# The MLP's input forms and low parts on VectorE, its quarters loaded at other times

## What is computed

```python
xn = rmsnorm(x, norm_mix_g)
z = xn @ w_in                                  # q | k | v | u | gate
attn_out = sink_attend(q, k, v, ...)           # windows of 128, chunks of 64
lru_out = gelu(gate) * rglru(u, ...)           # causal conv, then a scan
h = x + concat(attn_out, lru_out) @ w_out
hn = rmsnorm(h, norm_ffn_g)
y = h + square(relu(hn @ w_up)) @ w_down
y_out = rmsnorm(y, final_norm_g)
```

## Time and profile before

| | |
|---|---|
| median of three runs | 2179.25 us (2178.5 to 2181.05) |
| profiled execution | 2178.8 us |
| its span | 2177.0 us |
| PE busy | 1991.7 us, 91% |
| PEld busy | 1887.9 us, 87% |
| DVE busy | 1535.1 us, 71% |
| ACT busy | 1012.1 us, 46% |
| POOL busy | 498.3 us, 23% |
| chain that ended last | PE 63%, DVE 11%, issue 9%, POOL 7%, DMA 5%, ACT 3% |
| DRAM traffic over the span | 375.36 MB read, 123.68 MB written, 229 GB/s |

### The profile page before, as it was taken

How to read it: one execution, slowest core, us unless ns; L and a number is a source line. 1 busy time by engine, 2 the same in 40 slices (tenths; PEclk the granted TensorE clock), 3 DMA queues, 4 the chain that set the end, 5 groups by cost and what they waited for, 6 DMA issues and landing times.

```text
span 2177.0 us, 34222 instructions
## 1 busy us (share of the span) xinstructions
PE 1991.7 (91%) x11669; PEld 1887.9 (87%) x11669; DVE 1535.1 (71%) x2167; ACT 1012.1 (46%) x1967; POOL 498.3 (23%) x411
## 2 busy tenths in 40 slices
PE   6789889988898689999999889999999899999994
PEld 6778678777786489999999889999999799999994
DVE  7767777677679678878887866666666756666663
ACT  5555544644644355555555444433335433343431
POOL 3536565555666310100000401000002100000000
PEclk9889999999998799999999999999999899999997
DMA  6767677666755289988999887768878667777771
GB/s 176 222 175 230 179 220 227 199 218 186 239 176 172 77 305 308 320 289 289 344 324 293 267 279 245 231 204 264 270 222 270 225 197 218 216 216 216 219 213 63
DMA packets 396538, 500.91 MB, mean 230 GB/s; under 512 B 27498, under 2 KB 301450, under 8 KB 396394
## 3 DMA queue, kind: packets, MB, share of 16 engines
q1 hardware_dynamic: 394698, 493.38, 72.7%
q0 software_dynamic: 1696, 5.67, 0.8%
HBM read 375.36 MB, written 123.68 MB: 229 GB/s over the span
## 4 chain that ended last, share of the span: by engine, by line
PE 63%; DVE 11%; issue 9%; POOL 7%; DMA 5%; ACT 3%; SPq 1%; POOLq 0%; DVEq 0%; ACTq 0%
PE results L2065 19%; PE scores_a L2065 13%; PE tail L2065 13%; PE results L1849 9%; PE aux L2065 7%; DVE w_lo L1399 2%; PE aux L1969 1%; DMA s_scratch<-w_hi 1%; POOL xrow L930 1%; POOL prob L961 1%; DVE w_lo L1524 1%; POOL xrow L932 1%; POOL xrow L934 1%; DMA out<-hid_y 1%; POOL third L932 1%
## 5 line engine op out<-in xcount | busy, mean ns | idle before, releaser
L1081 ACT ACTIVATE w_hi<-w_raw 128x512 fp32r<-128x512 f32 (+1 forms) x360 | 241.0, 691 | 395.0 <-PE results L2065 174.8
L1524 DVE TENSOR_TENSOR w_lo<-w_raw,w_hi 128x512 fp32r<-128x512 f32 (+1 forms) x360 | 293.6, 829 | 49.9 <-ACT w_hi L1081 49.4
L1849 PE MATMUL results<-xg_hi,w_hi 128*128 128x448 f32 (+1 forms) x560 | 215.0, 384 | 27.4 <-DVE w_lo L1399 21.4
L1849 PE MATMUL results<-xg_lo,w_hi 128*128 128x448 f32 (+1 forms) x560 | 202.6, 362 | 0.0
L1849 PE MATMUL results<-xg_hi,w_lo 128*128 128x448 f32 (+1 forms) x560 | 202.4, 361 | 0.0
L2065 PE MATMUL results<-hn_hi,w_hi 128*128 128x348 f32 x576 | 189.4, 329 | 13.3 <-DVE hcur L1734 8.0
L1017 ACT ACTIVATE w_hi<-raw 128x1024 fp32r<-128x1024 f32 x110 | 116.3, 1058 | 167.3 <-PE results L1849 162.8
L1399 DVE TENSOR_TENSOR w_lo<-raw,w_hi 128x1024 fp32r<-128x1024 f32 x110 | 158.1, 1437 | 48.2 <-ACT w_hi L1017 48.0
L2065 PE MATMUL results<-hn_hi,w_lo 128*128 128x348 f32 x576 | 187.6, 326 | 0.0
L2065 PE MATMUL results<-hn_lo,w_hi 128*128 128x348 f32 x576 | 187.5, 326 | 0.0
L2065 PE MATMUL scores_a<-hn_hi,w_hi 128*128 128x348 f32 x480 | 156.3, 326 | 4.6 <-DVE hn_lo L1514 2.8
(11 more groups left out here) (275 smaller groups left out, 5726.1 us busy)
## 6 DMA issues: line engine op xcount, KB each, us to landing
w_lo<-s_scratch SPq DMA_DIRECT2D x128, 512.0 KB, 4.4
w_hi<-s_scratch SPq DMA_DIRECT2D x256, 256.0 KB, 3.6
w_raw<-in_w_up SPq DMA_DIRECT2D x144, 256.0 KB, 4.6
w_raw<-in_w_down SPq DMA_DIRECT2D x144, 256.0 KB, 4.3
raw<-in_w_in SPq DMA_DIRECT2D x70, 512.0 KB, 5.0
w_raw<-s_raw SPq DMA_DIRECT2D x64, 512.0 KB, 5.6
s_scratch<-w_lo SPq DMA_DIRECT2D x64, 512.0 KB, 5.8
s_scratch<-w_hi SPq DMA_DIRECT2D x128, 256.0 KB, 6.0
```

What stands on the lines that cost most here:

```text
L1081: nc.scalar.activation(ring(w2_hi, u, ks[0], len(ks)), raw_slots(u, ks[0], len(ks)), ACT.Copy)\
L1524: nc.vector.tensor_tensor(w2_lo[u.s][:, PHYS[ks[0]]:PHYS[ks[0]] + len(ks), :], raw_slots(u, ks[0], len(ks)), ring(w2_hi.bitcast(F32), u, k ...
L1849: last = nc.tensor.matmul(out, wt, x(kx), start=(start and i == 0 and part == 0), stop=(stop and i == len(ks) - 1 and part == 2))
```

## The change

- **Engine.** `input_form` goes from POOL to DVE for all three blocks, and so do low parts 6 and 4. POOL keeps nothing of `hn`. The semaphore `hn_lo_p` goes; `hn_lo_v` counts seven low parts, in the order 0 to 6.
- **Last mixing block, SP and POOL.** Quarters 0, 3 and 1 are loaded at q = 7, after that unit's sums have been moved, and quarter 2 at q = 8 as before. A unit's sums are now moved ahead of its quarter loads. Sum store 5 is issued at n = 18 instead of 17; sums step 5 is made after round 2's scaling instead of round 1's.
- **Last mixing block, DVE.** The two halo copies are left out there. In the four pairs of output halves stand form c (pair c), low part c - 1 (from pair 1 on), and weight low parts of unit 0 in pairs 2 and 3. Low parts 3 to 6 follow in unit 0.
- **Blocks 0 and 1, SP.** Quarters 0, 1 and 2 are loaded after products 0, 3 and 5 of unit 29, each one alone; quarter 3 (in `held`) at product 0 of unit 30, with the waits for unit 29's hidden parts.
- **Blocks 0 and 1, DVE.** Form 0 stands in unit 30, forms 1 to 3 and low parts 0 and 1 in unit 31, low parts 2 to 6 in unit 0 of the next block.
- **ACT.** High parts in the order 0, 5, 3, 1, 2, 6, 4; 0, 5 and 3 in unit 30, the others in unit 31.

```diff
-IORD = (0, 1, 2, 3, 6, 4, 5)
+IORD = (0, 5, 3, 1, 2, 6, 4)
...
-              "last": {9: 0, 11: 1, 12: 2, 15: 3, 16: 4, 17: 5}}
+              "last": {9: 0, 11: 1, 12: 2, 15: 3, 16: 4, 18: 5}}
...
-            "last": {"ix0": (0,), "ix1": (1, 2), "scan": (3, 4), 1: (5,)}}
+            "last": {"ix0": (0,), "ix1": (1, 2), "scan": (3, 4), 2: (5,)}}
...
-                    if blk.last and q == 6:
+                    move_sums(blk, n)
+                    if blk.last and q == 7:
                         sp.wait_ge(freed, 2 + uses + Z1)
                         sp.wait_ge(lru_lo, blk.before(2) + 2)
-                        for k in (0, 1, 3):
+                        for k in (0, 3, 1):
                             sp.dma_start(hn_slot(k), h_quarter(h_dram, 0, k)).then_inc(hn_in[k], 16)
                     if blk.last and q == 8:
                         sums_stored(blk)
                         sp.dma_start(hn_slot(2), h_quarter(h_dram, 0, 2)).then_inc(hn_in[2], 16)
-                    move_sums(blk, n)
...
-                if i == 30 and k == 0:
-                    last_up = Unit(UN * (b - 1) + 29)
-                    sp.wait_ge(prod_done, last_up.product(6))
-                    sp.wait_ge(hid_lo_done, hid_split(last_up.n, 5))
-                    sp.wait_ge(t_done, 3 * last_up.n + 2)
+                if i == 29 and k in (0, 3, 5):
+                    q = {0: 0, 3: 1, 5: 2}[k]
                     for h in range(2):
                         sp.wait_ge(ht_out[h], 16 * KT * b)
-                    for q in (0, 3, 2, 1):
-                        sp.dma_start(hn_slot(q), h_quarter(hn_dram[b - 1], 0, q)).then_inc(hn_in[q], 16)
+                    sp.dma_start(hn_slot(q), h_quarter(hn_dram[b - 1], 0, q)).then_inc(hn_in[q], 16)
+                if i == 30 and k == 0:
+                    n = Unit(UN * (b - 1) + 29).n
+                    sp.wait_ge(hid_lo_done, hid_split(n, 5))
+                    sp.wait_ge(t_done, 3 * n + 2)
+                    sp.dma_start(hn_slot(3), h_quarter(hn_dram[b - 1], 0, 3)).then_inc(hn_in[3], 16)
...
-                if u.i == 0:
-                    for k in hn_low_pool(u.b):
-                        input_low(u.b, k)
...
-                link(nc.vector.tensor_copy(kT[:, 0:CHUNK], kT[:, end:end + CHUNK]))
-                nc.vector.tensor_copy(vT[:, 0:CHUNK], vT[:, end:end + CHUNK]).then_inc(halo_done, 1)
+                if not blk.last:
+                    link(nc.vector.tensor_copy(kT[:, 0:CHUNK], kT[:, end:end + CHUNK]))
+                    nc.vector.tensor_copy(vT[:, 0:CHUNK], vT[:, end:end + CHUNK]).then_inc(halo_done, 1)
...
-                    if blk.last and couple == 2:
-                        weights_low(0, 0)
-                    if blk.last and couple < 3:
-                        input_low(0, IORD[couple])
+                    if blk.last:
+                        if couple >= 2:
+                            weights_low(0, couple - 2)
+                        input_form(0, couple)
+                        if couple >= 1:
+                            input_low(0, couple - 1)
...
                 if u.i == 0:
-                    input_low(u.b, 3)
-                    input_low(u.b, 5)
+                    for k in range(2 if u.b else 3, 7):
+                        input_low(u.b, k)
```

99 lines of the change are left out of this document (45 added, 54 removed).

## The result

The changed kernel takes 2145.55 us, median of three runs (2143.62 to 2146.69), against 2179.25: a ratio of 0.9843, interval 0.982 to 0.9865, or 33.7 us less. The forecast was 2141, its range 2133 to 2153. The profiled execution is the slowest of the three, 2146.7 us with a span of 2144.9.

A forecast was written before the change was run, and what follows sets the result against it. PE, the busiest engine, was taken to lose time only at three places where the MLP gets its input. Gains 19 + 12 + 9 = 40, less 1.5, gave 38.5 off 2179.25: 2141 us, range 2133 to 2153.

The forecast's parts named there:

- A1: Last mixing block: reordered sums and quarter loads remove PE's wait for POOL's scaling and the slow clock; gain 9.6 us.
- no wait for POOL's scaling above 2 us: Sign at the last mixing block: PE never waits more than 2 us for POOL's scaling of the probabilities.
- A2: Last mixing block: forms off POOL and no halo copy cut PE's 9.06 us wait to about 1; gain 8.
- A form on DVE: Length of an input form on DVE: bounds 1.60 and 3.40 us, 1.60 taken; at 3.40 the pairs lose 5 us.
- A3: Last mixing block's output halves, with moved DVE work: 21.0 us instead of 22.6, gain 1.5; 0 if the clock falls.
- Unit 0: After the last sum: doesn't move; a start of product 6 other than 21 us behind it would show the prediction wrong.
- B: End of block 0, units 30 to 32: 14.9 us lost, 2.5 to 3 of them stay; gain 12.
- the landing of the store of high parts: End of block 0: taken 2 us over the 6.0 median, so that ACT no longer makes DVE late.
- rival 1: New waits on quarter or store loads, unit 29 on or last mixing block, 0 to 4 us each: 2149; chance 0.17.
- The laying-out of forms and low parts in DVE's order: End of block 0: delays of 0.4 us before product 6, and 1 each at products 0 and 1 of unit 32.
- three signs: End of block 0: ACT's store wait below 2 us, PE's waits 3 us in sum, clock at its upper level.
- C: End of block 1: of 11.7 us lost, 0.65 + 1.0 + 1.1 stay; gain 9.

The follow-up runs named there:

- e4: The kernel before with only the changed order of sums, stores and quarter loads in the last mixing block; 2169.2 us.
- e5: The changed kernel with sum step 5 made behind round 1's scaling again instead of round 2's; 2149.1 us.
- e3: The changed kernel with the four input forms back on GpSimd in the last mixing block alone; 2155.1 us.
- e2: The changed kernel with the two halo copies of the last mixing block back; 2143.5 us.
- e0: The changed kernel run again without any edit, on the same chip as e12; 2147.5 us.
- e9: The changed kernel with the residual's loads moved from the start of unit 0 to behind its product 4; 2144.4 us.
- e12: As e7, with three weight loads of unit 32 behind unit 31's stores (block 0), residual's loads behind unit 0's first store; 2141.9 us.
- e7: As e1, with form 0 also moved on DVE from unit 30 to behind unit 31's first two additions; 2147.0 us.
- e1: The changed kernel with ACT's input high parts 5 and 3 behind all weight high parts in unit 30; 2150.0 us.
- e6: As e1, with all four quarters loaded at product 0 of unit 30 and high part 0 behind the weight high parts; 2152.1 us.

## Why the prediction was right, and where its sizes were off

**What bounds, and A1.** Right in place and size: 9.6 us forecast, 9.6 in the profile, 9.5 in e4 alone. Its sign, no wait for POOL's scaling above 2 us, was wrong all the same: the 2.30 us of the last round stood there before too. One bound was too tight: the landing of the step's data took 7.2 us as the upper end, and e5 measured 9.0. That did no harm, since the loads went out at 701.37 and POOL found the data there at 709.96, "by 711" as the sum has it.

**A2.** Right: 8 forecast, 8.2 measured. It is POOL's doing: e3 brings back 5.1 of it, and the copy beside a form, which e3 doesn't have, made up the 3.1 left. The prediction booked these 3.1 us to leaving the copies out; by e2 that gives nothing once the forms are away.

**A form on DVE** takes 1.60 us, the value taken; the other end of 3.40 was needed nowhere.

**A3.** The failed step is the clock: the sum took the output halves at the upper level, since only 1 us of wait was left in front; for a fall of the clock it had put the gain at 0. Busy time and clock of the stretch (length, busy us of PE, PEld, DVE, ACT, POOL, granted clock, DMA share, GB/s):

```profile
724.00:732.00 8.00, 4.70 (x27) 3.05 (x25) 7.59 (x20) 2.75 (x13) 1.73 (x2) 1.00 0.23 79
732.00:736.00 4.00, 2.09 (x11) 1.27 (x12) 2.82 (x7) 2.15 (x5) 0.35 (x1) 0.84 0.00 2
736.00:740.00 4.00, 4.00 (x12) 3.56 (x11) 1.03 (x1) 1.18 (x1) 0.00 (x0) 0.50 0.36 86
740.00:744.00 4.00, 4.00 (x18) 3.63 (x18) 1.25 (x2) 0.63 (x1) 0.00 (x0) 0.80 1.05 277
```

After the last rounds, in which PE is busy for about half of the time, the first 16 matmuls run at the lower level. In e0, the same program, the eight halves take 23.0 us instead of 24.55, so the gain is -0.4 there and -1.9 here, and no profile of this order has the 1.5. The wait of half 14, 1.27 us, came where the sum had put it (1.2).

**Unit 0** was said not to move; its product 6 starts 19.5 us behind the first product instead of 21.2, which the prediction itself had named as a sign of being wrong. What ACT waits for was named rightly (e9, e12), but the store's landing isn't a fixed distance from the last sum: 18.1 us behind the unit's first product before, 16.4 after.

**B.** The term that failed is the landing of the store of high parts: 8 us were taken, two over the median of all such stores, "with which ACT no longer makes DVE late". The store that ACT waits for here took 10.3 us in the changed kernel, and 10.9 in the trace of before, where the prediction could have read it. By e7 10.3 us leave PE 2.52 us late, and some 7.8 was the point; so the argument was right and the size wrong. In the changed kernel itself ACT makes DVE late by 2.31 us even ahead of that, since it stands 3.73 us before the third quarter. The two quarter waits (3.73 us on ACT, 2.59 on DVE in e1) are rival 1's mechanism; it had named DVE and the store, not ACT, and priced it with 0 to 4 us at this place, where 4.5 were missing. What the earlier loading does for the store was put too high: by e6 it is worth 1.6 us at place B, within the scatter. The laying-out of forms and low parts in DVE's order was right to 0.3 us: 0.57, 0.76 and 0.89 for 0.4, 1 and 1. And about 1 us is the clock: e0, the same program with a wait of 2.19 us there, took 36.39. So three signs of the prediction failed here: ACT's wait for the store below 2 us (4.19), PE's waits of 3 us in sum (4.0), and the clock at its upper level.

**C.** Right: 9 forecast, 8.9 measured.

**Behind the transposes** the forecast had nothing, and 3.9 us were lost. Five low parts in a row put DVE's first yout 8.0 us behind the first transpose, where it was 6.5; the prediction looked only at the products which these parts feed, and not at what is queued behind them on DVE:

```profile
1216.54 7.68 DVE L1497 TENSOR_TENSOR hn_lo<-hn_raw,hn_hi 128x1392 fp32r<-128x1392 f32 x5
...
1225.35 1.28 DVE L1673 SCALAR_TENSOR_TENSOR yout<-aux,ystat,gfin 116x1024 f32<-116x1024 f32 x1
```

PE's wait for yout before the third pair of transposes grew from 1.30 to 2.00 us behind block 0 and from 1.65 to 2.79 behind block 1. How much of the 3.9 us that is, and how much the clock's, stays open: the stretch to unit 30 took 416.0 to 421.1 us in the kernels with the forms of blocks 1 and 2 on DVE, 415.1 and 417.0 in before and e4.

The terms that were too high (A3 3.4, B 4.5, behind the transposes 3.9) sum to 11.8; those too low (unit 0 and the units after it 3.4, the start 0.4) give back 3.8. The total came out 8 below the sum of 40, of which 1.5 had been taken off. So the time lies in the range, and part of that is luck: errors of 11.8 us one way were met by 3.8 the other, and by the 1.5 taken off.

## What to carry to other kernels

Before work is spread over two engines, look how long an instruction takes on either while the other runs: here VectorE's instructions took nearly four times as long beside a few long ones of GpSimd, and taking the same work onto the fuller engine was the gain. When a wait is removed, list what else would have ended within a few us of it on every engine in order, and for a moved instruction also what is queued behind it there; at place B three waits in a row took each other's place. Where transfers fill the queues, a landing is priced by that transfer's own landing at that place (10.9 us in the trace of before), not by a median over the run (6.0).

## What the runs showed that was not expected

A load of 696 KB took 11 us to land in unit 30 of block 0 (1179.72 to 1190.84, and 1183.53 to 1194.49 in e1), and the store of 256 KB that ACT waits for there 8.6 to 10.7 us with the forms on DVE. It differs by 1.7 us between two executions of one program (10.3 in the changed kernel, 8.6 in e0). PE's clock differs between executions of one program at the same place: the output halves of the last mixing block took 23.0 or 24.5 us in nine profiles of the same order there, depending on how many matmuls ran at the lower of its two levels.
